# Probabilities times v: the transposed probabilities become the weights, v's pairs the moving operand

## The reference

```python
s = jnp.einsum("bthd,btkd->bthk", qb, kg).astype(jnp.float32) * (Dh ** -0.5)
s = jnp.where(valid[:, :, None, :], s, -jnp.inf)
p = jax.nn.softmax(s, axis=-1).astype(vg.dtype)
return jnp.einsum("bthk,btkd->bthd", p, vg)
```

## Time and profile before

| what | value |
|---|---|
| median of 3 runs (lowest, highest) | 595.83 us (595.68, 599.75) |
| the profiled execution | 598.7 us, of it 597.0 us span in the trace |
| PE busy | 537.3 us (90%) |
| PE weight loads busy | 444.7 us (75%) |
| DVE busy | 424.0 us (71%) |
| ACT busy | 389.5 us (65%) |
| POOL busy | 211.1 us (35%) |
| L1728, product with v | 288 matmuls of 256 columns |
| L1750, fold | 128 matmul instructions of 64 columns |
| L1054, copy of the product | 32, 12.2 us busy |

### The profile page before, as it was taken

One profiled execution on the slowest core, in us unless ns is written; L12 is line 12 of the kernel. 1 busy time (PEld: TensorE's weight loads), 2 busy tenths in 40 slices (PEclk: granted clock), 3 DMA queues, 4 the chain that ended last, 5 costly groups with the idle time before them and its releaser, 6 DMA issues.

```text
span 597.0 us, 8273 instructions
## 1 busy us (share of the span) xinstructions
PE 537.3 (90%) x2758; PEld 444.7 (75%) x2758; DVE 424.0 (71%) x994; ACT 389.5 (65%) x691; POOL 211.1 (35%) x190
## 2 busy tenths in 40 slices
PE   0489988999999999999999967589999999999995
PEld 0477767888687777778888755478898989888874
DVE  4775659788989889997888775645576656664532
ACT  4583534564599899988898856655657566656631
POOL 6522052031436253488464001751312030314222
PEclk9999998999999999989999977889999999999998
DMA  8992293141111112133353060020101010101021
GB/s 306 397 340 87 55 287 109 44 107 36 29 44 36 36 36 70 36 106 107 106 124 88 5 278 1 4 103 2 71 1 72 1 64 8 42 31 71 1 72 70
DMA packets 19658, 51.98 MB, mean 87 GB/s; under 512 B 4128, under 2 KB 5152, under 8 KB 19616
## 3 DMA queue, kind: packets, MB, share of 16 engines
q1 hardware_dynamic: 19616, 51.45, 27.1%
HBM read 37.81 MB, written 4.19 MB: 70 GB/s over the span
## 4 chain that ended last, share of the span: by engine, by line
PE 71%; DVE 10%; ACT 8%; issue 5%; POOL 3%; DMA 2%; SPq 1%; DVEq 0%; POOLq 0%; ACTq 0%
PE pair L1556 26%; PE pair L1704 14%; PE pair L1728 6%; PE pair L1741 5%; PE pair L1525 4%; PE pair L1611 3%; PE pair L1612 2%; PE pair L1655 2%; DVE score_sb L1376 2%; PE pair L1764 2%; PE pair L1750 2%; PE pair L1646 1%; PE pair L1647 1%; DMA x_sb<-in_x 1%; PE pair L1502 1%
## 5 line engine op out<-in xcount | busy, mean ns | idle before, releaser
L1464 DVE TENSOR_TENSOR pt_lo<-pair,pt_hi 128x512 fp32r<-128x512 f32 (+3 forms) x96 | 50.5, 554 | 70.7 <-ACT pt_hi L1066 70.1
L1556 PE MATMUL pair<-h_hi,w_hi 128*128 128x512 f32 x304 | 98.8, 406 | 0.0
L959 ACT ACTIVATE bias_sb<-score_sb,tinies 128x1024 bf16<-128x1024 f32 (+2 forms) x93 | 95.7, 1032 | 4.0 <-DVE tinies L1245 3.8
L1556 PE MATMUL pair<-h_lo,w_hi 128*128 128x512 f32 x304 | 95.1, 394 | 0.0
L1556 PE MATMUL pair<-h_hi,w_lo 128*128 128x512 f32 x304 | 94.5, 392 | 0.0
L1231 DVE TENSOR_SCALAR_CACHE_REDUCE bias_sb<-score_sb,tinies 128x640 bf16<-128x640 f32 (+2 forms) x93 | 72.4, 801 | 0.8
L760 POOL TENSOR_SCALAR w_hi<-w_raw 128x1024 fp32r<-128x1024 f32 (+1 forms) x22 | 23.3, 1059 | 136.0 <-DMA w_raw<-in_w_tiles 116.2
L1556 PEld LDWEIGHTS pair<-h_hi,w_hi 128*128 128x128 f32 x304 | 56.7, 190 | 14.6 <-issue 4.5
L1556 PEld LDWEIGHTS pair<-h_hi,w_lo 128*128 128x128 f32 x304 | 57.9, 191 | 12.5
L1556 PEld LDWEIGHTS pair<-h_lo,w_hi 128*128 128x128 f32 x304 | 57.6, 190 | 12.5
L1066 ACT ACTIVATE pt_hi<-pair 128x512 fp32r<-128x512 f32 (+3 forms) x96 | 43.5, 488 | 24.5 <-PE pair L1741 22.2
(11 more groups left out here) (216 smaller groups left out, 1306.0 us busy)
## 6 DMA issues: line engine op xcount, KB each, us to landing
w_raw<-in_w_tiles SPq DMA_DIRECT2D x21, 512.0 KB, 4.0
ada<-in_ada_w SPq DMA_DIRECT2D x16, 512.0 KB, 12.2
x_sb<-in_x SPq DMA_DIRECT2D x8, 512.0 KB, 9.7
ada_g<-in_ada_w SPq DMA_DIRECT2D x8, 512.0 KB, 6.0
qs<-half_hi SPq DMA_DIRECT2D x16, 256.0 KB, 3.9
qs<-half_lo SPq DMA_DIRECT2D x16, 256.0 KB, 4.9
wo_raw<-in_w_out SPq DMA_DIRECT2D x8, 512.0 KB, 6.5
x_res<-in_x SPq DMA_DIRECT2D x8, 512.0 KB, 3.3
```

The costliest lines, as they stand in the source:

```text
L959: nc.scalar.activation(junk[i], score_sb[:, SCORE_OFF[i]:SCORE_OFF[i] + keys_of(i)], ACT.Sign, bias=cand[:, c:c + 1], scale=-1.0, accum_ou ...
L1464: nc.vector.tensor_tensor(pt_lo[:, 4 * b:4 * b + nc4, hh, :], psum[use % 2][:, 0:nc4 * P].rearrange("p (c q) -> p c q", q=P), f32(pt_hi[:, ...
L1556: ins = nc.tensor.matmul(psum[banks[half]][0:width, :], w[b][:, k, 0:width], hh[:, k, half * HALF:(half + 1) * HALF], start=(k == 0 and p ...
```

## The change

The product with v changes its roles. The weights are now one chunk of one head of `pt_hi` or `pt_lo` (128 keys by 128 queries), and `v_pair[:, c, :]` moves through them, 128 columns. The result for one head is `[query, v part and dimension]`, and the two heads lie side by side in columns 0 to 255 of bank 2. The queries are on partitions already. ACT's copy `pv_sb` and the fold are no longer executed. DVE adds v's two parts itself: it scales the high part of both heads into `o_sb`, waits for that, and then for each head adds the scaled low part with a second instruction that reads PSUM and `o_sb`. `LAG_O` falls from `LAG_T + 3` to `LAG_T + 2`, so that this work stands in step 2q + 3, the step of the product, and not in the next one. PE's waits for `pv_ok` and `fold_ps` go, DVE's wait for `fold_ps` becomes one for `pv_ps`; PE's wait for `o_ok` of the pair before stays.

```diff
-LAG_O = LAG_T + 3
+LAG_O = LAG_T + 2
...
-                if g >= LAG_PV and (g - LAG_PV) % 2 == 0 and (g - LAG_PV) // 2 < 32:
-                    q = (g - LAG_PV) // 2
-                    act.wait_ge(pv_ps, q + 1)
-                    if q >= 2:
-                        act.wait_ge(fold_ps, q - 1)
-                    nc.scalar.activation(pv_sb[q % 2][:, :, :], psum[2][:, 0:256].rearrange("p (h q) -> p h q", h=2), ACT.Copy).then_inc(pv_ok, 1)
...
                     link(nc.vector.reciprocal(rinv[:, :], rsum[:, r0:r0 + 2]))
-                    dve.wait_ge(fold_ps, q + 1)
+                    dve.wait_ge(pv_ps, q + 1)
                     if pr == 0 and ti:
                         dve.wait_ge(t_ps, PT_USE["Y", ti - 1, 0] + 1)
-                    c0 = 256 + 128 * (q % 2)
-                    nc.vector.tensor_tensor(o_sb[:, pr * P:(pr + 1) * P].rearrange("p (h d) -> p h d", h=2),
-                                            psum[2][:, c0:c0 + P].rearrange("p (h d) -> p h d", h=2),
-                                            rinv[:, :].unsqueeze(2).to_broadcast([P, 2, HD]), ALU.mult).then_inc(o_ok, 1)
+                    pv = psum[2][:, 0:256].rearrange("p (h e d) -> p h e d", h=2, e=2)
+                    o2 = o_sb[:, pr * P:(pr + 1) * P].rearrange("p (h d) -> p h d", h=2)
+                    link(nc.vector.tensor_tensor(o2, pv[:, :, 0, :], rinv[:, :].unsqueeze(2).to_broadcast([P, 2, HD]), ALU.mult))
+                    for hh in range(2):
+                        ins = nc.vector.scalar_tensor_tensor(o2[:, hh, :], pv[:, hh, 1, :], rinv[:, hh:hh + 1], o2[:, hh, :], ALU.mult, ALU.add)
+                    ins.then_inc(o_ok, 1)
...
                     if q:
-                        pe.wait_ge(pv_ok, q)
                         pe.wait_ge(o_ok, q)
-                    for c in range(i + 1):
-                        for p, t in enumerate((pt_hi, pt_lo)):
-                            ins = nc.tensor.matmul(psum[2][:, 0:256], v_pair[:, c, :], t[:, c, :, :].rearrange("p h q -> p (h q)"),
-                                                   start=(c == 0 and p == 0), stop=(c == i and p == 1))
+                    for hh in range(2):
+                        for c in range(i + 1):
+                            for p, t in enumerate((pt_hi, pt_lo)):
+                                ins = nc.tensor.matmul(psum[2][:, hh * P:(hh + 1) * P], t[:, c, hh, :], v_pair[:, c, :],
+                                                       start=(c == 0 and p == 0), stop=(c == i and p == 1))
                     ins.then_inc(pv_ps, 1)
...
-                if g >= LAG_O and (g - LAG_O) % 2 == 0 and (g - LAG_O) // 2 < 32:
-                    q = (g - LAG_O) // 2
-                    pe.wait_ge(pv_ok, q + 1)
-                    if q >= 2:
-                        pe.wait_ge(o_ok, q - 1)
-                    for hh in range(2):
-                        c0 = 256 + 128 * (q % 2) + HD * hh
-                        ins = nc.tensor.matmul(psum[2][:, c0:c0 + HD], pv_sb[q % 2][:, hh, :], fold[:, :], start=True, stop=True)
-                    ins.then_inc(fold_ps, 1)
```

More of the change, by code:

```diff
@@ L589, in layer_kernel @@
         pv_ps = sem("pv_ps")
-        pv_ok = sem("pv_ok")
-        fold_ps = sem("fold_ps")
         rinv_ok = sem("rinv_ok")
```

## The result

The changed kernel takes 627.65 us (4 runs, 622.85 to 628.57) against 595.75 of the kernel before (4 runs). The ratio estimated from the runs is 1.0496, 95% interval 1.0457 to 1.0535: 5% slower. (The two medians alone give 1.0535, its upper end; the profiled spans give 1.049.) The forecast was 611.5 us, range 604 to 618: the direction was right, the size (+16) half of what came (+31.9).

The account below looks back on a forecast made before the run. PE was taken to bound from about 396 us; pace +26.7, fold -10.3, stalls -0.7 and lost cover +0.1 gave +15.8, with +0.5 for tiles 1 and 0 about +16 us. Forecast 611.5 us on the median, range 604 to 618.

Parts of the forecast that it names:

- What bounds: From 400 us PE is busy 20.0 of 20 us at full clock; there relief of ACT is worth nothing.
- Pace of the product, +26.7: Full part: 264 matmuls at 0.119 us go, 528 at 0.11 us come, +26.7 us.
- The rivals with hidden loads: Product's weight loads hidden: 0.06 us per matmul, 585.5 us, 4%; half hidden: 0.08 to 0.085, 596 to 599 us, 5%.
- The fast-load rule: Skill's rule for the product's weights: 128 non-FP32 weights load fast, so no extra cost; the forecast counted f32r as slow.
- Fold, -10.3: Full part: 24 folds on PE at 0.43 us each go, -10.3 us.
- DVE has 8 us free of 20 in the full part ... so this is hidden: 0: DVE's new instructions, about 0.5 us per pair, cost 0 in the full part; up to 12 us were DVE full.
- Earlier `o_sb`, -0.7: PE's stalls in tiles 2 and 3 shrink with `o_sb` a step earlier: -0.7 us, between none and 2.
- Tiles 1 and 0, +0.5 with bounds of -3 and +4: Before the output projection: longer products, folds and copies gone, longer DVE work; sum taken as +0.5 us.
- the signs of being wrong: Starts 0.06 to 0.08 us apart, PE idle in front of the product, or a different granted clock in tiles 1 and 0.
- The terms for tiles 1 and 0 (+2.3, -1.5, +0.5): Tiles 1 and 0: products on the path +2.3 us, folds and copies gone -1.5, DVE's longer work +0.5.
- the first rival: Product's loads always hidden, 0.06 us per matmul, so the folds' 10.3 us are a gain: 585.5 us, 4%.
- DVE's work lands on the path or the clock falls: DVE's new work on the path, or a lower clock in tiles 1 and 0: 617 to 624 us, 6%.

Follow-up runs that it names:

- e2: Kernel before with each 256-column product matmul made as two of 128, one per head; copy, fold and DVE's work as before: 627.34 us.
- e12: e6 with only v's high part moving, 64 columns instead of 128 per product matmul, v's low part left out of the result: 628.4 us.
- e6: Changed kernel with DVE's block that writes `o_sb` moved ahead of `pt_lo` in the same step: 619.0 us.
- e8: Tiles 1 and 0 as in the kernel before, the other six with the new product and `o_sb` ahead of `pt_lo`: 613.79 us, ratio 1.0296.
- e11: Changed kernel with `o_sb` ahead of `pt_lo` and three useless 512-column matmuls in each of steps 4 to 15: 616.51 us.
- e5: Changed kernel without DVE's two instructions that add v's low part and the wait ahead of them: 620.08 us.
- e3: Hybrid: tiles 1 and 0 as in the kernel before, the other six tiles as in the changed kernel: 621.4 us.
- e9: Changed kernel with three useless 512-column matmuls added in each of steps 4 to 15: 623.08 us.
- e10: Kernel before with three useless 512-column matmuls added in each of steps 4 to 15: 597.41 us, ratio 0.998 to 1.003.
- e4: Hybrid: tiles 1 and 0 as in the changed kernel, the other six tiles as in the kernel before: 599.72 us, ratio 1.004.

## Why the forecast was right and wrong

- **What bounds: right.** PE bounds from 396 us on in the kernel before, and all terms of PE came out; no run shows a gain from what ACT gave back (the copies, 12.2 us). In the kernel after PE also has its waits for `q_free`, which the forecast had not.
- **Pace of the product, +26.7: right.** 0.11 us per matmul. e2 measures this term alone at +25.6, or +26.4 without the wait of 0.8 that it lost. It came from three kinds of rows: a single short matmul, the transposes, and the loads' own starts. The rivals with hidden loads are out.
- **The fast-load rule: rightly set aside.** The Trainium skill, "TensorE: Matmul & The Clock Gate", section "Weight-path perf modes", has fast loads for 128 weights that are not FP32. With f32r weights this kernel shows 0.11 us per load with 128 columns (after, e2) and with 64 (e12), so the trace does not have f32r among the fast ones.
- **Fold, -10.3: right.** e6, e8 and e11 have full parts of 209.8 to 210.3, e2 has 219.2: -8.9 to -9.4, with 0.9 us of waits for `q_free` left in them, so about -10 by itself (an estimate; no run takes out the fold alone).
- **"DVE has 8 us free of 20 in the full part ... so this is hidden: 0": wrong.** This is the step that failed, with the term for tiles 1 and 0 below as the second. It measured 7.3 us (after against e6), 5.6 of it for the two new instructions and the wait ahead of them alone (e5). The size of the work was right (0.91 us from the reciprocal to `prob`, against 0.16 + 0.29 for the two instructions that were there and my 0.5 for the new ones). What was wrong is the argument from the busy share, and "the step's `prob` behind it is wanted by the transposes of the next PE step" looked at only one of those that wait. In an even step `q_free` stands behind `prob`, and PE needs `q_free` for its bank right after the next scores. I had also seen the product get longer without asking what is late by it: in the odd step the transposes come behind the product, so `pt_lo` ends late by all that the product grew, and everything on DVE behind it starts from there. Looking for the free time at the place, and not over the stretch, would have led there.
- **Earlier `o_sb`, -0.7: PE's one wait for it in the full part (0.8 us) is gone,** but with the wrong price beside it: one step earlier *behind* `pt_lo` is where it does harm. e2, which leaves `o_sb` in its old step, has lost the wait too, so the longer product alone is enough for that.
- **Tiles 1 and 0, +0.5 with bounds of -3 and +4: wrong.** It was +5.5 between the two profiles, and 6 between the medians of e3 and the kernel after. I had priced the products at either clock but taken the clock itself as given, though a different clock there stands among the signs of being wrong, and it came: 0.76 to 0.62. The short matmuls bring it, for e2 has it without any other change. That the lower clock is what costs the time is made likely by e9 and not shown, since e10 gained nothing. How much is due to it stays open (2 us by e4, 4.6 by e9, 6 by e3 and after).
- **Slips in the sums.** The terms for tiles 1 and 0 (+2.3, -1.5, +0.5) make +1.3, and +0.5 was taken without a price for the difference. 615 less 2.9 is 612.1, not 611.5, and the first rival's sum makes 585.6, not 585.5. None of it changes the outcome: with +1.3 and 612.1 the forecast is 613.
- **The profiled execution of before** was 2.9 us above the median, that of after at the median. The spans differ by 29.1, the medians by 31.9; the forecast's sum on one run could not see that.
- **The rivals.** "DVE's work lands on the path or the clock falls", 6%, 617 to 624 us, is what happened, with its first half shown (e5, e6) and its second likely (e9). I had given it a price with too little on either half: DVE's 7 us in the full part lie within the "up to 12 us over 24 pairs" of the text, and that end of an unknown cost was not carried into the range; with it and the upper bound of tiles 1 and 0 the range would have reached 627 (611.5 + 12 + 3.5), still just short of 627.65.

## What to carry to other kernels

Where weights are f32 or f32r, count weight loads: a run of matmuls that each bring 128 new columns of weights costs 0.11 us apiece here, whether 64 or 128 columns move through (256 take 0.12), so put the wide operand on the moving side. Before calling an engine's new work hidden, find the idle place in which it fits and put it there: the same instructions cost 7 us behind a late `pt_lo` and about 1 ahead of it. When a stage gets longer on one engine, ask what stands behind it in the same step on every engine, and who waits for the last of that.

## What the runs showed of the hardware

- A busy PE can lose its clock. In e12 PE was busy 20.00 of 20 us from 460 to 480 us and the granted clock fell to 0.80 on average, from the end of a product of 32 matmuls with 64 columns each; with 128 columns and the same loads (e6, e8, e11) it stayed at 1.00. With half the columns the kernel took 9 us more. The numbers in PE differ too, so the columns are the likely cause and not the shown one.
- Useless matmuls can raise the clock: 36 of 512 columns in tiles 1 and 0 brought it from 0.62 to 0.83 in the changed kernel, whose median fell by 4.6 us, and from 0.76 to 0.86 in the kernel before, whose time stayed.
- f32r weights of 128 by 128 come 0.11 us apart at full clock whether 64 or 128 columns move (3.49 and 3.53 us for 32 matmuls), and which operand is the weights makes no difference (2.19 us for 20 in e2 and in the kernel after).
